# Up biases by one product with a 64-row selector, and expert rows gathered with the selection stationary and then transposed

## The reference, cut to what matters

```
logits = t @ w_router + b_router ; top_vals, top_idx = top_k(logits, 4) ; gates = softmax over the 4
for e in range(32):
    hu  = t @ w_gu[e] + b_gu[e]                     # 1024 -> 2048
    glu = minimum(hu[:, :1024], 7) ; lin = clip(hu[:, 1024:], -7, 7)
    act = glu * sigmoid(1.702 * glu) * (lin + 1)
    y   = y + gates[:, e:e+1] * (act @ w_dn[e] + b_dn[e])
```

## Time and profile before

| | us |
|---|---|
| median of 3 runs | 1108.92 |
| lowest, highest | 1108.81, 1109.72 |
| the profiled execution's own time | 1109.2 |
| its span, first to last instruction | 1107.0 |
| PE busy | 1069.9 (97%) |
| DVE busy, ACT busy | 258.4 (23%), 144.7 (13%) |
| DMA, mean over the span | 390 GB/s |
| PE's waits for up weights, for down weights | 24.1, 7.2 |

### The profile page before, as it was taken

One profiled execution on the slowest core, in us unless ns is written; L12 is line 12 of the kernel. 1 busy time (PEld: TensorE's weight loads), 2 busy tenths in 40 slices (PEclk: granted clock), 3 DMA queues, 4 the chain that ended last, 5 costly groups with the idle time before them and its releaser, 6 DMA issues.

```text
span 1107.0 us, 12035 instructions
## 1 busy us (share of the span) xinstructions
PE 1069.9 (97%) x5130; PEld 445.0 (40%) x5130; DVE 258.4 (23%) x531; ACT 144.7 (13%) x283; POOL 17.3 (2%) x45
## 2 busy tenths in 40 slices
PE   9999999999999999999999899998989999999898
PEld 5485563434343434343434232333333344433234
DVE  4274241231121212121212121111212021212122
ACT  4134341100000000000000000000000100000022
POOL 2001100000000000000000000000000000000000
PEclk9999999999999999999999999999999999999999
DMA  9943589999999999999999999999999999999981
GB/s 348 368 163 123 242 350 384 427 428 427 427 427 429 427 427 426 429 428 427 427 429 429 427 426 429 429 428 426 427 428 426 427 428 428 427 428 427 425 342 38
DMA packets 43004, 431.89 MB, mean 390 GB/s; under 512 B 6231, under 2 KB 6751, under 8 KB 17606
## 3 DMA queue, kind: packets, MB, share of 16 engines
q1 hardware_dynamic: 42736, 431.07, 93.1%
q10 hardware_dynamic: 214, 0.04, 0.0%
HBM read 430.04 MB, written 1.06 MB: 389 GB/s over the span
## 4 chain that ended last, share of the span: by engine, by line
PE 69%; DMA 30%; DVE 0%; issue 0%; ACT 0%; ACTq 0%; DVEq 0%
PE hu L1096 23%; DMA ring<-in_w_gate_up 22%; PE po L1126 15%; DMA ring<-in_w_down 8%; PE aux L1043 5%; PE hu L723 5%; PE hu L729 3%; PE aux L1051 3%; PE hu L739 2%; PE hu L1088 2%; PE hu L765 1%; PE aux L1303 1%; PE po L1103 1%; PE aux L1076 1%; PE hu L1126 1%; PE po L1303 1%
## 5 line engine op out<-in xcount | busy, mean ns | idle before, releaser
L1096 PE MATMUL hu<-ring,num_xg 128*64 128x512 f32 x1920 | 431.6, 596 | 24.1 <-DMA ring<-in_w_gate_up 24.1
L1096 PEld LDWEIGHTS hu<-ring,num_xg 128*64 128x64 f32 x1920 | 131.5, 137 | 304.2 <-issue 257.2
L1126 PE MATMUL po<-ring,arena 128*64 128x512 f32 x976 | 219.3, 600 | 7.2 <-DMA ring<-in_w_down 7.2
L1126 PEld LDWEIGHTS po<-ring,arena 128*64 128x64 f32 x976 | 67.9, 137 | 154.3 <-issue 139.9
L1674 DVE TENSOR_SCALAR arena<-hu 128x512 f32<-128x512 f32 x31 | 21.4, 692 | 432.0 <-PE hu L1096 432.0
L1650 DVE TENSOR_TENSOR arena<-arena,aux 128x512 f32<-128x512 f32 x58 | 37.3, 684 | 133.3 <-PE aux L1051 121.4
L1043 PEld LDWEIGHTS aux<-num_xg,big 128*128 128x128 f32 x512 | 58.4, 192 | 13.0 <-issue 13.0
L1043 PE MATMUL aux<-num_xg,big 128*128 128x128 f32 x512 | 61.4, 278 | 0.0
L723 PE MATMUL hu<-ring 128*128 128x512 f32 x128 | 56.7, 595 | 0.0
L1997 ACT ACTIVATE hu<-arena 128x512 f32<-128x512 f32 x31 | 18.6, 601 | 249.0 <-DVE arena L1674 249.0
L1663 DVE TENSOR_SCALAR arena<-iota_s,posm,gates 128x128 f32<-128x128 f32 x64 | 17.9, 342 | 118.2 <-PE po L1126 115.3
(11 more groups left out here) (275 smaller groups left out, 606.5 us busy)
## 6 DMA issues: line engine op xcount, KB each, us to landing
ring<-in_w_gate_up SPq DMA_DIRECT2D x125, 2048.0 KB, 36.0
ring<-in_w_down SPq DMA_DIRECT2D x60, 2048.0 KB, 36.1
ring<-in_w_in SPq DMA_DIRECT2D x6, 2048.0 KB, 16.2
ring<-in_w_gate_up SPq DMA_DIRECT2D x6, 1024.0 KB, 7.7
ring<-in_w_out SPq DMA_DIRECT2D x2, 2048.0 KB, 12.2
ring<-in_w_down SPq DMA_DIRECT2D x4, 1024.0 KB, 37.6
ring<-in_w_ple_gate SPq DMA_DIRECT2D x2, 2048.0 KB, 34.1
ring<-in_w_in SPq DMA_DIRECT2D x4, 512.0 KB, 6.5
```

The lines of the kernel that those rows point to most:

```text
L1096: last = mm(hu[n * SLOTS:(n + 1) * SLOTS, 2 * e + b, :], rows_of[:, k, e * SLOTS:(e + 1) * SLOTS], w[:, o:o + NB], start=first, stop=(k == ...
L1126: last = mm(bank[n * SLOTS:(n + 1) * SLOTS, :], actT[:, f, h * SLOTS:(h + 1) * SLOTS], w[:, o:o + NB], start=(h == 0 and f == 0), stop=(h ...
```

## The change

Three things change.

- **Up bias.** The 32 x 1024 halves of `b_gate_up` are laid out anew in `bias`: rows 0 to 31 hold the first 512 columns of glu and of lin, rows 32 to 63 the second 512 of each. `up_bias` has two products (`b` = 0, 1) for each expert, each with a stationary operand of 64 rows x 128 columns: `bias_rows`, which ACT writes (`selector`), one copy of 64x128 behind each sigmoid and two ahead of the loop. PE waits for it (`bias_rows_ready`).
- **Gather in pairs 0 to 12** (so for the rows of pairs 1 to 13). `gather_rows(c)` takes the one-hot as the stationary operand and 512 features of `h2` as the moving one; the output has slots on partitions. ACT copies it from PSUM to `slot_rows`, PE transposes it in blocks of 128x128 (`row_transposes`) back to `aux`, where DVE reads it as before. The second half's transposes stand behind `act_transposes` and `up_bias`. Pairs 13 and 14 still use `gather_half`.
- **Waits.** PE waits for ACT's copies (`rows_out`) ahead of each half's transposes, and ACT for `rows_ps`.

```diff
@@ SP @@
-            for j in range(2):
-                sp.dma_start(bias[32 * j:32 * j + E, :], b_gate_up[0][:, j * D:(j + 1) * D]).then_inc(late_loaded, 16)
+            for n in range(HALVES):
+                sp.dma_start(bias[E * n:E * n + E, :].rearrange("e (b c) -> e b c", b=2), bias_src[n]).then_inc(late_loaded, 16)
@@ PE @@
+            def gather_rows(c):
+                for tt in range(TT):
+                    last = mm(aux[:, c, :], onehot[:, tt, :, :].rearrange("p e s -> p (e s)"), h2[:, tt, c * NB:(c + 1) * NB],
+                              start=(tt == 0), stop=(tt == TT - 1))
+                last.then_inc(rows_ps, 1)
+
+            def row_transposes(c):
+                for k in range(4 * c, 4 * c + 4):
+                    last = tr(aux[:, c, k % 4 * P:(k % 4 + 1) * P], slot_rows[:, k * P:(k + 1) * P], ident[:])
+                last.then_inc(xg_ps, 1)
...
             def up_bias(e, expert, first):
                 for b in range(2):
-                    for n in range(HALVES):
-                        mm(hu[n * SLOTS:(n + 1) * SLOTS, 2 * e + b, :], expert_rows(b, expert),
-                           bias[32 * b:32 * b + E, n * NB:(n + 1) * NB], start=first, stop=False, skip_group_check=True)
+                    mm(hu[:, 2 * e + b, :], bias_rows[:, expert % 2, :, :].rearrange("p n s -> p (n s)"),
+                       bias[0:HALVES * E, b * NB:(b + 1) * NB], start=first, stop=False, skip_group_check=True)
...
+                    pe.wait_ge(bias_rows_ready, experts + (2 * pair + 2))
                     up_bias(1, 2 * pair + 1, False)
...
-                        for c in range(2):
-                            gather_half(c, aux[:, c, :])
+                        if pair < NEXT_PAIR:
+                            for c in range(2):
+                                gather_rows(c)
+                            pe.wait_ge(rows_out, ps * (2 * NEXT_PAIR) + (2 * pair + 1))
+                            row_transposes(0)
+                        else:
+                            for c in range(2):
+                                gather_half(c, aux[:, c, :])
                         pe.wait_ge(act_ready, experts + (2 * pair + 2))
                         act_transposes(2 * pair + 1)
+                        pe.wait_ge(bias_rows_ready, experts + (2 * pair + 3))
                         up_bias(0, 2 * pair + 2, True)
+                        if pair < NEXT_PAIR:
+                            pe.wait_ge(rows_out, ps * (2 * NEXT_PAIR) + (2 * pair + 2))
+                            row_transposes(1)
@@ ACT @@
+            def selector(expert):
+                both = ident[0:HALVES * E, 0:HALVES * E].rearrange("p (n e) -> p n e", n=HALVES)
+                a.copy(bias_rows[:, expert % 2, :, :], both[:, :, expert:expert + 1].to_broadcast([HALVES * E, HALVES, SLOTS]))\
+                 .then_inc(bias_rows_ready, 1)
+
+            act.wait_ge(xg_ps, 2)
+            selector(0)
+            selector(1)
...
                         a.activation(hu[:, 2 * e, :], gated(2 * pair + e), ACT.Sigmoid, scale=ALPHA).then_inc(sig_ready, 1)
+                        selector((2 * pair + e + 2) % E)
...
                         sigmoid(1)
+                        if pair < NEXT_PAIR:
+                            for c in range(2):
+                                act.wait_ge(rows_ps, ps * (2 * NEXT_PAIR) + (2 * pair + c + 1))
+                                a.copy(slot_rows[:, c * NB:(c + 1) * NB], aux[:, c, :]).then_inc(rows_out, 1)
                         transposed_act(1)
```

More of the change, by code:

```diff
@@ L198, in hybrid_layer @@
         onehot = num_xg[:, NB:NB + S].rearrange("p (t e s) -> p t e s", t=TT, e=2)
+        bias_rows = num_xg[0:HALVES * E, NB + S:NB + 2 * S].rearrange("p (i n s) -> p i n s", i=2, n=HALVES)
         gatesT = num_xg[64:64 + E, NB + S:NB + 2 * S]
@@ L206, in hybrid_layer @@
         xg0 = early[:, 2048:2048 + K * P].rearrange("p (k s) -> p k s", k=K)
+        slot_rows = early[:, 2048:2048 + D]
         out_s = [num_xg[:, 0:NB], early[:, 4 * S:4 * S + NB]]
@@ L329, in hybrid_layer @@
         ghotT_ready = sem("ghotT_ready")
+        rows_ps = sem("rows_ps")
+        rows_out = sem("rows_out")
         xg_ps = sem("xg_ps")
         xg_ready = sem("xg_ready")
+        bias_rows_ready = sem("bias_rows_ready")
         glu_ready = sem("glu_ready")
@@ L351, in hybrid_layer @@
         dn_src = w_down[0].rearrange("e (h p f) n -> e h p (f n)", h=2, f=4)
+        bias_src = b_gate_up[0].rearrange("e (b n c) -> n e b c", b=2, n=HALVES)
         x_src = x[0].rearrange("(t p) d -> p t d", p=P)
@@ L1078, in ple @@
                 last.then_inc(ple_ps, 1)
-            def expert_rows(part, expert):
-                return sel_part[32 * part:32 * part + E, expert:expert + 1].to_broadcast([E, SLOTS])
             def up_bias(e, expert, first):
                 for b in range(2):
-                    for n in range(HALVES):
-                        mm(hu[n * SLOTS:(n + 1) * SLOTS, 2 * e + b, :], expert_rows(b, expert),
-                           bias[32 * b:32 * b + E, n * NB:(n + 1) * NB], start=first, stop=False, skip_group_check=True)
+                    mm(hu[:, 2 * e + b, :], bias_rows[:, expert % 2, :, :].rearrange("p n s -> p (n s)"),
+                       bias[0:HALVES * E, b * NB:(b + 1) * NB], start=first, stop=False, skip_group_check=True)
             def up_block(e, rows_of, w, k, first, halves=range(2)):
@@ L1155, in up_chunk @@
                         if c == 2 and e == 0 and pair == 0:
+                            pe.wait_ge(bias_rows_ready, experts + 1)
                             up_bias(0, 0, False)
```

## The result

| | before | changed |
|---|---|---|
| median, 15 runs each | 1109.19 us | 1112.21 us |
| lowest, highest | 1108.06, 1111.52 | 1111.57, 1113.10 |
| ratio, 95% interval | | 1.0026 (1.0020 to 1.0033) |
| span of the profiled execution | 1107.0 | 1110.0 |

A forecast was written before the change was run, and what follows sets the result against it. The weights' DMA stream was taken as the bound, with PE's work free up to a cover. 23.4 + 16.3 = 39.7 us against 37.5 to 39.2 left 1.4, so 1110.4 us; own range 1108.9 to 1111.1, full range 1108.6 to 1115.0.

The forecast's parts named there:

- What bounds the kernel: In the pairs, the DMA stream of weights is at its limit, 423 to 432 GB/s, whatever PE's load.
- The cover: PE work hidden over the pairs: 31.3 us of waits plus 6.2 of restarts, 37.5 us, or 39.2 with the clock's part.
- that clock row: One chunk behind a 1.61 us wait took 5.35 us at granted clock 0.57; 1.70 us that may not recur.
- The bias: Up bias, 32 times: 1.88 us instead of 1.02, 0.86 longer each, bounds 0.70 to 0.89.
- The gather: Pairs 0 to 12, gather to down: 7.07 us instead of 5.27, 1.80 more, bounds 1.3 to 1.9.
- The round trip through ACT: ACT's copies ahead of PE's row transposes: waits priced at 0, at most 0.3 us a pair.
- PE's term: PE's added work, 23.4 us in 13 pairs plus 16.3 for 19 other biases, 39.7 against the cover.
- Is the queue still fed?: Slots released 3.5 us later at 233 us; transfers would land after 6.7 us, near the edge, recovering 2.7 us a pair.
- rival (d): Queue runs dry in pairs 0 and 1; stream ends 1.8 to 3.6 us later, 1111.6 us; chance 0.04.
- the sign of being wrong that I had named: The DMA stream with gaps near 235 us, one of the signs listed as showing the forecast wrong.
- The sum: Whole kernel: 39.7 us added against the cover leaves 0.5 to 2.2 us, middle 1.4; time 1110.4 us.
- rival (a): PE becomes the bound by several us, added work 41.7 to 45.6 us; 1111.4 to 1117, middle 1114; chance 0.40.

The follow-up runs named there:

- e7_shared_tiles: Kernel before, with the new bias layout and four 32x64 bias products, glu and lin of one half sharing rows and columns of the array; 1111.22 us, ratio 1.0018.
- e2_gather_only: Changed kernel with the up bias as before, keeping the new gather, ACT's copies and the row transposes in pairs 0 to 12; 1109.79 us, ratio 1.0005.
- e6_extra45: Kernel before, with the activation's four transposes issued five times instead of once at both places of pairs 2 to 14; 1120.49 us, ratio 1.0103.
- e3_delay_pair0: Kernel before, with the activation's four transposes issued five times instead of once at both places in pair 0; 1113.17 us, ratio 1.0038.
- e8_reordered: Changed kernel, with the up bias and the second half's row transposes of pair 0 moved behind down; 1115.15 us, ratio 1.0055.

## Why the prediction was right, and where it was not

- **What bounds the kernel**: right. PE's work is free up to a cover, and the stream of weights stays at 427 to 430 GB/s whether PE idles or not. Without any bias the kernel gains 0.1%.
- **The cover**: forecast 37.5 to 39.2 us, measured 39.1. The waits alone (31.3) would have been wrong by 8; with the restart of 0.22 us behind each wait and the chunk at the lower clock the sum comes to 39.2. In the changed kernel that clock row is gone: the granted clock is 1.00 in every 10 us of the pairs.
- **The bias**: forecast 1.88, measured 1.91 us. The reason, four products side by side against full-width ones in turn, was borne out by `e7_shared_tiles`.
- **The gather**: forecast 7.07 from its start to down, measured 7.05. The gather proper took 3.63, not 3.59, and the bias 0.03 more; the first transposes took 0.44, not 0.48, the last 0.59, not 0.64. An early pair was forecast at 56.0 us and took 56.0 (the bias of the second expert starts at 244.63 and 300.64).
- **The round trip through ACT**: forecast at nothing, and no idle time stands before either group of transposes. `e2_gather_only` costs nothing measurable.
- **PE's term**: forecast 39.7 against 37.5 to 39.2; measured 40.1 against 39.1. By it alone the kernel would be 1.0 us slower.
- **Is the queue still fed?**: this step failed. I had the delay right (3.5 us forecast at 233 us; measured 3.4, both there and at the slot that came at 221.1 instead of 217.7), called it near the edge, and then priced it at zero; as rival (d) I gave it 1.8 to 3.6 us and a chance of 0.04. It was what happened: the stream's end came 2.7 us later, and the sign of being wrong that I had named, gaps in the DMA stream, appeared, at 221 us instead of 235. Two readings were wrong. I looked at the transfers issued from 230 to 240 us and not at the one at 217.7, the first behind 12 us without an issue. And I compared their 6.7 us with "the smallest value in the pairs", 7.0. That 7.0 belongs to a transfer of half the size, issued at 170.9 into a nearly empty queue (229 and 242 GB/s in the windows of 2 us from 170 and 172):

```profile
ring<-in_w_down SPq DMA_DIRECT2D x1, 1024.0 KB, 7.0
```

  Between 180 and 1000 us no transfer of 2 MB in the kernel before lands in less than 10.2 us. The one issued at 221.1 in the changed kernel landed after 7.3 us, and that was already a gap. A smallest landing time can be the mark of a dry queue; it is no proof that the queue can bear it.
- **The sum**: it had PE's excess over the cover as its only term, 1.4 us, and the stream's loss at nothing. They are two limits of which the later one counts: PE's end (+1.0) and the stream's end (+2.7). The measured 3.0 is the stream's. It lies above the forecast's own range (to 1111.1) and inside the full one (to 1115.0), but the full range reached that far for rival (a), more work on PE, which is not what happened. That the full range held is in part luck.

Why pair 0 is sensitive can be read in the program and was not tried apart: the eleventh slot, in `arena`, is not refilled after its one use. PE works off that chunk from 210.5 to 214.0 us, behind the gather, the transposes and the bias, and its end triggers no load; so none is issued for 12 us (before: 205.4 to 217.7), while in pair 1 the longest interval is 8.8 us (259.6 to 268.4).

## What to carry to other kernels

If a stream of transfers sets the pace and another engine has slack, ask two questions of added work: does its total exceed the slack, and does it delay a release at a place where the queue is short? The first is a sum over the whole kernel. The second is asked place by place: here 3.9 us of work in pair 0 cost 4.1 us, while 37.8 us in the pairs from 2 on were free. Look for the longest time without an issue, and compare a landing time only with transfers of the same size. And count what stands side by side in the array, not instructions: merging four products of 32x64 into two of 64x128 halved the calls and nearly doubled the time, from 1.02 to 1.91 us.

## What was not expected of the hardware

- A dip in the queue cost more than the empty time. In the changed kernel only 220 to 224 us has the gap, 1.8 us worth; another 2 us are missing from 228 to 244, where the DMA engines are reported busy (shares of 0.83 to 1.12) and move 311 to 434 GB/s. The cause was not found. A similar dip (402 GB/s from 220 to 240) occurred in `e6_extra45` with issues as before.
- What the windows lack and what the last wait shows agree only to about 1 us: 3.9 us against 2.7 in the changed kernel, 4.1 against 4.0 in `e3_delay_pair0`, 6.2 against 5.3 in `e8_reordered`. Where the rest comes back is not shown.
- Repeated float32 transposes of 128x128 cost 0.121 us each (1.94 us for 16), not the 0.107 that a quarter of the 0.429 us for 512 columns would give.
